# Narrow weight sums moved behind the plain low halves, and six 512 KB reloads at given slots, in a fp32r decoder layer

## The reference

```python
h = rms_norm(x, norm_mix)
proj = h @ w_in                      # three head groups: GLA, mLSTM, spatial gating
x = x + mix @ w_out                  # mix: the outputs of the three groups
hf = rms_norm(x, norm_ffn)
gate, up = split(hf @ w_gu, 2)       # w_gu: 2048 x 11264
x = x + (silu(gate) * up) @ w_down   # w_down: 5632 x 2048
return rms_norm(x, norm_final)
```

## Time and profile before

| | us |
|---|---|
| median of 3 runs (1097.21 to 1098.8) | 1097.41 |
| the profiled execution | 1097.72 |
| its span, first to last instruction | 1096.0 |
| TensorE busy | 1084.9 |
| DVE busy | 888.4 |
| ACT busy | 598.8 |
| granted TensorE clock, share of full | 0.999 |

### The profile page before, as it was taken

How to read it: one execution, slowest core, us unless ns; L and a number is a source line. 1 busy time by engine, 2 the same in 40 slices (tenths; PEclk the granted TensorE clock), 3 DMA queues, 4 the chain that set the end, 5 groups by cost and what they waited for, 6 DMA issues and landing times.

```text
span 1096.0 us, 13959 instructions
## 1 busy us (share of the span) xinstructions
PE 1084.9 (99%) x5071; PEld 902.9 (82%) x5071; DVE 888.4 (81%) x1092; ACT 598.8 (55%) x736; POOL 40.7 (4%) x68
## 2 busy tenths in 40 slices
PE   9999999999999999999999999999999999999997
PEld 7897889888888888888888888888888878888885
DVE  5556866688756557999999999999998999899896
ACT  5655545555545445555655555556556555646553
POOL 2600000000010000000000000000000000000000
PEclk9999999999999999999999999999999999999999
DMA  8665646565546675656566566556666856666663
GB/s 290 214 199 168 186 131 179 161 173 154 181 163 235 188 253 171 204 185 210 189 199 214 165 208 206 185 184 209 210 192 197 301 190 215 203 200 209 200 224 117
DMA packets 110948, 215.39 MB, mean 197 GB/s; under 512 B 6957, under 2 KB 11633, under 8 KB 110001
## 3 DMA queue, kind: packets, MB, share of 16 engines
q1 hardware_dynamic: 108976, 205.36, 59.1%
q0 software_dynamic: 1632, 8.96, 2.2%
q10 hardware_dynamic: 288, 0.39, 0.1%
HBM read 210.49 MB, written 4.19 MB: 196 GB/s over the span
## 4 chain that ended last, share of the span: by engine, by line
PE 92%; DVE 4%; DMA 2%; issue 1%; ACT 1%; SPq 0%; POOLq 0%; POOL 0%; DVEq 0%; ACTq 0%
PE acc L1454 11%; PE acc L1455 11%; PE acc L1456 11%; PE acc L1735 10%; PE acc L1734 10%; PE acc L1736 10%; PE acc L1805 4%; PE acc L1807 4%; PE acc L1806 4%; PE mx L1734 3%; PE mx L1735 2%; PE mx L1736 2%; PE mx L1446 2%; PE mx L1805 1%; PE mx L1807 1%; PE mx L1806 1%
## 5 line engine op out<-in xcount | busy, mean ns | idle before, releaser
L786 DVE TENSOR_TENSOR w_lo<-raw,w_hi 128x1024 fp32r<-128x1024 f32 (+2 forms) x144 | 166.4, 1169 | 120.2 <-ACT w_hi L473 119.5
L473 ACT ACTIVATE w_hi<-raw 128x1024 fp32r<-128x1024 f32 (+2 forms) x143 | 143.2, 1013 | 135.4 <-PE acc L1456 129.0
L1734 PE MATMUL acc<-w_hi,hT_hi 128*128 128x512 f32 x460 | 179.9, 391 | 0.0
L1735 PE MATMUL acc<-w_lo,hT_hi 128*128 128x512 f32 x460 | 179.1, 389 | 0.0
L1736 PE MATMUL acc<-w_hi,hT_lo 128*128 128x512 f32 x460 | 179.0, 389 | 0.0
L1221 DVE TENSOR_TENSOR w_lo<-raw,w_hi 128x1024 fp32r<-128x1024 f32 (+1 forms) x160 | 173.3, 1119 | 2.8
L673 ACT ACTIVATE w_hi<-raw 128x1024 fp32r<-128x1024 f32 (+1 forms) x160 | 151.5, 978 | 36.7 <-PE acc L1736 21.8
L1454 PE MATMUL acc<-w_hi,hT_hi 128*128 128x512 f32 (+2 forms) x416 | 157.7, 379 | 0.0
L1456 PE MATMUL acc<-w_hi,hT_lo 128*128 128x512 f32 (+2 forms) x416 | 155.5, 374 | 0.0
L1455 PE MATMUL acc<-w_lo,hT_hi 128*128 128x512 f32 (+2 forms) x416 | 155.5, 374 | 0.0
L679 ACT ACTIVATE w_hi<-ff_sum 128x1024 fp32r<-128x1024 f32 x60 | 63.8, 1063 | 78.3 <-PE acc L1736 65.2
(11 more groups left out here) (317 smaller groups left out, 1682.5 us busy)
## 6 DMA issues: line engine op xcount, KB each, us to landing
raw<-in_w_gu SPq DMA_DIRECT2D x176, 512.0 KB, 4.2
raw<-in_w_down SPq DMA_DIRECT2D x88, 512.0 KB, 4.6
raw<-in_w_in SPq DMA_DIRECT2D x79, 512.0 KB, 4.0
raw<-in_w_out SPq DMA_DIRECT2D x32, 512.0 KB, 4.3
raw<-in_w_in SPq DMA_DIRECT2D x8, 272.0 KB, 2.8
raw<-in_w_in SPq DMA_DIRECT2D x8, 264.0 KB, 2.8
x<-in_x POOLq DMA_DIRECT2D x2, 1024.0 KB, 9.5
x_kept<-x POOLq DMA_DIRECT2D x2, 1024.0 KB, 7.3
```

Of the source, the lines that this page charges most:

```text
L786: dve.tensor_tensor(w_lo[:, slot, 0:UC * width], raw[:, slot, 0:UC * width], w_hi[:, slot, 0:UC * width].bitcast(F32), ALU.subtract).then_ ...
L1734: pe.matmul(o, a[0], w[0], start=first, stop=False)
L1735: pe.matmul(o, a[0], w[1], start=False, stop=False)
```

## The change

In the gate/up part and in the down part the two narrow sums of each seven move behind the low halves of v and v+1; the wide sum stays where it was. In seven 0 `act_sums` follows the wide sum directly. As the narrow sums read both raw tiles, the loads that overwrite these tiles get a second wait, for the narrow sums (`FF_SUMS_OF`, `SUMS_OF`). On POOL the three DMAs of 1024 KB become six of 512 KB, each behind a wait for a slot count in the down part: for the residual, left half, slots 17 and 29 (one for each block of tokens), right half, slots 67 and 77, and for the norm's weights slots 87 and 97. Semaphores are split in two accordingly.

```diff
+FF_SUMS_OF = {_i + d: 2 * _k + 2 for _kind, _k, _i, _v in FF_ORDER if _kind == "seven" for d in range(2)}
+SUMMED_AT = [_q for _kind, _half, _k, _q, _v in DOWN if _kind == "seven"]
+SUMS_OF = {_q + d: 2 * n + 2 for n, _q in enumerate(SUMMED_AT) for d in range(2)}
+BACK_AT = [V_DN + at for at in (17, 29, 67, 77, 87, 97)]
@@ load_ff
+                summed = FF_SUMS_OF.get(i - R)
+                if summed is not None:
+                    sp.wait_ge(sem("ff_w_sums"), (j - 1) * 2 * FF_SUMMED + summed)
                 sp.wait_ge(lo_ready, j * FF_SLOTS + (FF_BASE + FF_SLOT_OF[i - R] + 1))
@@ load_down
+                if q - R in SUMS_OF:
+                    sp.wait_ge(sem("w_sums"), SUMS_OF[q - R])
                 sp.wait_ge(lo_ready, SLOT_OF.get(q - R, V_DN + q - R - U_DN) + 1)
@@ gpsimd
-            for b in range(NB):
-                pool.dma_start(x1[:, b, :], x1_kept[b * P:(b + 1) * P, :]).then_inc(sem("x1_back"), 16)
-            pool.dma_start(nf_row[:, :], norm_final.partition_broadcast(P)).then_inc(sem("nf_loaded"), 16)
+            for h in range(2):
+                for b in range(NB):
+                    pool.wait_ge(unit_used, BACK_AT[2 * h + b])
+                    pool.dma_start(x1[:, b, h * 2 * GW:(h + 1) * 2 * GW],
+                                   x1_kept[b * P:(b + 1) * P, h * 2 * GW:(h + 1) * 2 * GW]).then_inc(sem(f"x1_back{h}"), 16)
+            for n in range(2):
+                pool.wait_ge(unit_used, BACK_AT[4 + n])
+                pool.dma_start(nf_row[:, n * 2 * GW:(n + 1) * 2 * GW],
+                               norm_final[n * 2 * GW:(n + 1) * 2 * GW].partition_broadcast(P)).then_inc(sem(f"nf_loaded{n}"), 16)
@@ ff_weight_sums: the two narrow sums become a function of their own
+            def ff_last_sums(j, i, k):
+                a, b = i % R, (i + 1) % R
                 dve.wait_ge(sem("ff_w_sums"), lin(j, 2 * FF_SUMMED, 2 * (k - FF_SUMMED) + 1))
@@ gate_up
                         ff_low(j, i + 1, v + 1, GW)
+                        ff_last_sums(j, i, k)
                         ff_sum_low(j, 0, v + 2)
@@ norm_row
-                dve.wait_ge(sem("nf_loaded"), 16)
+                dve.wait_ge(sem(f"nf_loaded{n // 2}"), 16)
@@ weight_sums: the two narrow sums become a function of their own
+            def last_sums(q, made):
+                a = q % R
                 dve.wait_ge(sem("actT_psum"), NG_FF)
@@ fold_banks
-                dve.wait_ge(sem("x1_back"), 16 * NB)
+                dve.wait_ge(sem(f"x1_back{half}"), 16 * NB)
@@ the order of DVE in the down part
                     down_low(v + 1, q + 1, GW)
+                    last_sums(q, 2 * sevens)
                     sum_low(v + 2, gate_s)
```

## The result

The changed kernel takes 1102.36 us (median of 6 runs, 1101.63 to 1103.14), the kernel before 1097.31 us beside it (6 runs). The ratio is 1.0044, with a 95% interval of 1.0033 to 1.0054: slower by 5.05 us. The forecast was 1098.5 us, within 1095.0 to 1102.5, so the time lies just inside the range and 3.9 us above the likeliest value, in the part that I had given 0.33. The profiled execution took 1101.63 us with a span of 1099.9; it is the lowest of the six, so the trace accounts for 3.9 of the 5.05 us.

What follows compares the result with a forecast made beforehand. TensorE, busy 1084.9 of 1096.0 us, was taken as the bound. The terms, +5.2 + 0.7 - 3.5 - 1.4 - 0.2 + 0.3 = +1.1 us, led to a forecast of 1098.5 us, range 1095.0 to 1102.5.

Steps and rivals of the forecast that it cites:

- Seven 0: Gate/up part: DVE waits for ACT ahead of `act_sums`, v+2 comes late; +5.2 us over groups 1 to 9, bounds 4.0 to 6.8.
- the start of the down part: All three TensorE waits on L1321 go, as no reload stands there and low v comes sooner: -1.4 us.
- the pieces: Six 512 KB reloads in the down part share DMA engines with weight loads: +0.3 us, bounds 0 and 1.1.
- Seven 2: Gate/up part: low v comes 1.46 us sooner, so TensorE's wait of 0.35 us goes in ten groups: -3.5 us.
- v+2 in seven 2: Gate/up part: v+2's low half has nothing to spare and is sometimes a little late: +0.7 us for ten groups.
- The held loads: Gate/up loads waiting for narrow sums: seven 1's wide sum waits up to 0.4 us, TensorE loses nothing, tile 11 barely in time.
- Rival 2: Tile 11's load lands late, so seven 2 keeps its wait in nine groups, 3.2 us: 1101.7 us; chance 0.18.
- The second half's first seven: Down part: the 0.7 us TensorE wait shrinks as the chain gets 0.12 us shorter: -0.2 us, bounds 0 and 0.5.
- rival 3: Down part: the six reload pieces collide with the loads of a seven, costing 2.3 us: 1100.5 us; chance 0.07.
- Rival 1: Seven 0's narrow sums are not missed, so the 5.2 us are not paid: 1093.3 us; chance 0.18.

Runs made afterwards that it cites:

- e2_ff_later: Against the kernel before, narrow sums moved behind the low halves only in sevens 1 and 2 of the gate/up part: 1094.83 us, ratio 0.9973; again 1094.82 us.
- e1_ff_all: Against the kernel before, only the gate/up half of the change, in sevens 0, 1 and 2; down part and reloads as before: 1101.8 us, ratio 1.0043.
- e6_one_ahead: As e1_ff_all, but in seven 0 the first narrow sum stays ahead of `act_sums`: 1094.77 us, ratio 0.9975 against the kernel before.
- e8_load_sooner: As e2_ff_later, but group 10 makes slot 20's low half ahead of `fold_gate`: 1094.19 us, ratio 0.997 against the kernel before; again 1093.9 us.
- e3_down_sums: Against the kernel before, only the down part's sums reordered, with SP's added waits there: 1097.62 us against 1097.61, ratio 1.0001.
- e4_pieces: Against the kernel before, only POOL's reloads split into six 512 KB pieces at their slots: 1097.25 us against 1097.61, ratio 0.9999.
- e5_undo_seven0: The changed kernel with seven 0's narrow sums back ahead of `act_sums` and no load waiting for them there: 1094.62 us, ratio 0.9977 against the kernel before.
- e7_copy_first: As e1_ff_all, but ACT makes its small copy ahead of the large one: 1102.14 us in a single run.

## Why the prediction was right, and where it was off

The direction was right, and so were the place and the mechanism of the loss, but the size was not: +1.1 us was forecast and +5.05 measured. That the time lies inside the range, by 0.14 us, is in part luck. Seven 0 cost more than its own upper bound of 6.8 us, the gain at the start of the down part, put at 0.9 us or more, doesn't show in any median, and a wait behind the last group was missing from the sum; allowances of up to 1.5 us for v+2 and 1.1 us for the pieces, which weren't used, made room for that.

**Seven 2: right.** The ten waits of 0.35 us are gone, and e2_ff_later shows the gain. From group 2 to group 9, by the starts of ACT's large copy, a group takes (774.14 - 477.43) / 7 = 42.39 us there, against (776.19 - 477.33) / 7 = 42.69 before: 0.31 us less, a little under the 0.35. Every trace with sevens 1 and 2 moved has one to three new waits of 0.16 to 0.39 us for a plain low half, of L1221's like, which the kernel before doesn't have; what they stand on was not tested.

**v+2 in seven 2: +0.7 us that weren't paid.** The chain was worked out right, only the allowance was idle. The timeline of DVE in the changed kernel has 626.91 for the wide sum and 631.11 for v+2, 4.20 us, against 586.05 - 581.84 = 4.21 by the prediction, and nothing waits there.

```profile
626.91 1.22 DVE L1258 TENSOR_TENSOR ff_sum<-raw 128x1024 f32<-128x1024 f32 x1
...
631.11 2.52 DVE L1242 TENSOR_TENSOR w_lo<-ff_sum,w_hi 128x1024 fp32r<-128x1024 f32 x2
```

**Seven 0: the mechanism was right, the size too small.** This is the term of the sum that was most mis-sized: 5.2 us, where the runs show 7.0. I had put 0.58 us a group. First matmul of v+2 in group 2 and in group 9 of the changed kernel, then the first of seven 2, groups 1 and 8, of the kernel before:

```profile
485.08 0.50 PE L1759 MATMUL mx<-w_hi,ff_hi 128*128 128x512 f32 x1 [0.46 <-DVE w_lo L1242]
...
787.54 0.49 PE L1759 MATMUL mx<-w_hi,ff_hi 128*128 128x512 f32 x1 [0.50 <-DVE w_lo L1242]
```

```profile
500.34 0.50 PE L1734 MATMUL mx<-w_hi,hT_hi 128*128 128x512 f32 x1
...
799.22 0.50 PE L1734 MATMUL mx<-w_hi,hT_hi 128*128 128x512 f32 x1
```

A group takes (787.54 - 485.08) / 7 = 43.21 us, and took (799.22 - 500.34) / 7 = 42.70. That is 0.51 us more, and with the 0.35 us that seven 2 gives back seven 0 costs 0.86. With eight groups at 0.86, and about 0.5 in group 1, where DVE starts 0.15 us sooner, it comes to 7.4 us in place of 5.2; e1_ff_all less e2_ff_later gives 7.0. A group of e1_ff_all takes (780.56 - 478.02) / 7 = 43.22 us by ACT's copies, 0.83 more than one of e2_ff_later, and this gives 7.1. So 7.0 is the better figure. Of the missing 0.28 us a group, 0.19 are the release of `act_sums`, which came 0.25 us after the end of ACT's copy in place of 0.06. I had taken the 0.06 from the release of TensorE by a low half. The other part is the release of TensorE by v+2: 614.81 - (613.46 + 1.22) = 0.13 us, in place of 0.06. The steps in between add up as predicted: from L1150 to v+2 5.08 us, predicted 611.75 - 606.66 = 5.09. Group 10 didn't wait there, as said.

**The held loads: as worked out.** The wide sum of seven 1 waits 0.32 us in this group (up to 0.4 predicted) and 0.24 to 0.70 in groups 2 to 9, that of seven 2 doesn't wait, and TensorE waits in a seven 1 once, for 0.16 us. Rival 2 fell: the ending that it described came about, but not by its mechanism. e6_one_ahead, with the loads still held for 1.1 us, is as fast as e2_ff_later.

**The end of the gate/up part: not in the sum.** I had looked for what is late next inside the group and not behind the last one. The wait for `act_tok` grew from 0.38 to 1.02 us in this trace, 0.64 us, so that group 10's gain of 0.35 us was given back and about 0.3 us more; in e1_ff_all it grew by 0.34. e8_load_sooner shows that the part above 0.33 us stood on the load of the down part's third tile.

**The start of the down part: -1.4 us that isn't there in the medians.** e3_down_sums and e4_pieces are both within 1.1 us of no change. I had taken the wait of one trace for the code's; the eight traces above, 0.46 us in the mean, speak for this, but the kernel before was profiled only once.

**The second half's first seven: about as predicted.** Its wait of 0.65 us (the earlier trace rows has it as 0.7) is 0.46 in the changed kernel and in e3_down_sums, 0.2 us less as I had said, but 0.80 in e5_undo_seven0, so a gain of this size is not shown.

```profile
978.24 0.19 PEld L1830 LDWEIGHTS acc<-w_hi,s_hi 128*128 128x128 f32 x1 [0.46 <-issue]
```

**The pieces: right in kind.** They cost nothing that the runs show (e4_pieces, -1.1 to +0.9 us); rival 3's 2.3 us fell with e4_pieces and e5_undo_seven0. Rival 1 fell with the result.

Put together: -3.5 for seven 2 and +0.6 behind the last group come to -2.9 us, and e2_ff_later measured -2.8. With +7.0 for seven 0, which is itself the difference of two runs, this gives the +4.2 us of e1_ff_all. What lies between that and the 5.05 us of the whole change is inside the intervals of both.

## What to carry to other kernels

Before moving an instruction out of the way of a late one, look at what follows it where it stood. If that waits for another engine, the instruction was filling the wait and cost nothing, and moving it makes what now stands behind it later: here 1.3 us of sums made v+2 1.2 us later, of which TensorE lost 0.8, as v+2 had been early; the same move can be right in one place (seven 2) and wrong in another (seven 0), so move it only where nothing waits behind it. A wait that appears once in a profile, unlike one that repeats in every pass of a loop, may be another size in the next execution, and a second trace of the same kernel is worth more than a finer sum.

## What the runs showed of the hardware

A vector instruction that had to wait for ACT started 0.24 to 0.26 us after ACT's end inside the hardware loop, and 0.10 us outside it (changed kernel; with the copies the other way round, 0.18 to 0.20 and 0.04 us, e7_copy_first). Inside, the queue's register work of about 0.1 us for that instruction began when the wait was over; where DVE came to it from other work, in the kernel before, the step took the usual 0.61 us, so the register work was hidden there. TensorE's wait at one place, for a low half that stands on a load, was anything from 0 to 1.24 us in eight executions of six kernels with the same code there, and 0.47 and 0.79 us in two executions of one kernel.
